# Dealing the closing products by a weight for each kind of attention slot, in place of equal shares of each step

## The reference, cut to what matters

```python
def sample_mixers(...):                       # 8 sequences, 4 new tokens each, 8192 past keys in 64 pages of 128
    o_a = dsa_attend(qa, qi, wi, qpos, kidx_all, gather_a, topk)      # branch A: keys chosen by an index score
    s = einsum('bqhmd,bshmd->bhmqs', q, k)    # branch B: scores of all past keys ...
    p = softmax(s); a = p[:, :, 0] - lam * p[:, :, 1]
    o = einsum('bhqs,bshe->bqhe', a, v)       # ... and the sum over all past values

def layer_out(h, o_a, o_b, g_a, g_b, p_i, tail):          # the closing products, for every token
    merged = sigmoid(g_a) * (o_a @ w_br_a) + sigmoid(g_b) * (o_b @ w_br_b)
    h = h + rmsnorm(merged @ w_out, attn_post_g)
    gate, up = split(rmsnorm(h, ffn_pre_g) @ w_gate_up, 2)
    h = h + rmsnorm((silu(gate) * up) @ w_down, ffn_post_g)
    return h + sigmoid(h @ w_ple_gate) * (p_i @ w_ple_proj)
```

## Time and profile before

| | |
|---|---|
| median of 3 runs | 3071.83 us (3071.17 to 3082.03) |
| the profiled execution, its own time | 3076.28 us |
| its span | 3074.7 us |
| PE busy | 2809.1 us, 91% of the span |
| DVE, ACT, POOL busy | 1398.5, 588.3, 676.6 us |
| granted TensorE clock, mean | 0.967 |
| woven stage | from about 1050 us to the end |

### The profile page before, as it was taken

The page is one execution under the profiler, slowest core; times in us unless marked ns, Lnnn a source line. Parts: engine busy times, 40 slices in busy tenths (PEclk is TensorE's granted clock), DMA queues, the critical chain, the costliest instruction groups (busy, mean ns, idle before and its releaser), DMA issues.

```text
span 3074.7 us, 69131 instructions
## 1 busy us (share of the span) xinstructions
PE 2809.1 (91%) x26846; PEld 1974.9 (64%) x26846; DVE 1398.5 (45%) x2685; ACT 588.3 (19%) x1285; POOL 676.6 (22%) x1190
## 2 busy tenths in 40 slices
PE   7998979999888598999988999999889899999898
PEld 5774434566566466667766666666666666776798
DVE  2336858997577545434344453343334532102211
ACT  2441113100566301101011110011110201001101
POOL 0131002100300000133333343433324334430000
PEclk9999989999899899999999999999899999999999
DMA  6566229521600576899898988988999987664586
GB/s 223 167 203 209 83 68 328 169 70 63 221 12 8 151 245 218 269 337 308 306 347 293 332 297 300 325 301 304 308 316 321 305 306 243 219 224 130 195 269 202
DMA packets 411138, 706.88 MB, mean 230 GB/s; under 512 B 67745, under 2 KB 225665, under 8 KB 410690
## 3 DMA queue, kind: packets, MB, share of 16 engines
q1 hardware_dynamic: 325042, 468.81, 46.3%
q0 software_dynamic: 75456, 232.86, 22.6%
q10 hardware_dynamic: 10320, 0.84, 0.3%
HBM read 659.90 MB, written 90.40 MB: 244 GB/s over the span
## 4 chain that ended last, share of the span: by engine, by line
PE 52%; DMA 4%; issue 3%; DVE 2%; ACT 1%; SPq 1%; POOLq 1%; DVEq 1%; POOL 0%; ACTq 0%
PE sa_t L1614 40%; PE sa_s L1969 4%; PE sa_o L2032 3%; DMA sa_ring_va<-cache_a_kv 2%; PE sa_s L1979 1%; PE sa_stat L2009 1%; ACT sa_prob_t L2110 1%; PE sa_o L2036 1%; DMA tw_x<-gate_t 1%; POOLq L1911 1%; DMA tw_w<-packed 1%; PE sa_t L1584 0%; DVE tw_rstd L1689 0%; DVEq L1697 0%; DMA sa_ring_k<-cache_b_kv 0%
## 5 line engine op out<-in xcount | busy, mean ns | idle before, releaser
L1614 PE MATMUL sa_t<-tw_z,tw_w 128*128 128x304 f32 (+1 forms) x3328 | 783.2, 393 | 7.2 <-issue 3.2
L1614 PEld LDWEIGHTS sa_t<-tw_z,tw_w 128*128 128x128 f32 x3328 | 572.3, 192 | 189.8 <-issue 42.3
L1912 POOL DMA_DIRECT2D sa_ring_v<-cache_b_kv x512 | 275.2, 537 | 1113.0 <-PE sa_o L2036 759.1
L1614 PE MATMUL sa_t<-tw_x,tw_w 128*128 128x304 f32 (+1 forms) x1920 | 453.0, 393 | 22.8 <-DMA tw_w<-packed 13.0
L2149 DVE STREAM_TRANSPOSE sa_key_b<-sa_ring_k 128x2048 f32<-128x2048 f32 x128 | 295.0, 2307 | 267.7 <-PE sa_s L1969 202.7
L1614 PEld LDWEIGHTS sa_t<-tw_x,tw_w 128*128 128x128 f32 x1920 | 330.9, 192 | 126.9 <-issue 32.5
L1913 POOL DMA_DIRECT2D sa_ring_va<-cache_a_kv x512 | 274.1, 535 | 54.1 <-issue 24.5
L462 PE MATMUL pr_acc<-pr_w,pr_u_t 128*128 128x512 f32 (+1 forms) x640 | 258.9, 549 | 5.2 <-DVE pr_row L651 5.2
L978 PE MATMUL sel_g<-sel_u,sel_gw 128*128 128x352 f32 x768 | 227.5, 459 | 0.0
L978 PEld LDWEIGHTS sel_g<-sel_u,sel_gw 128*128 128x128 f32 x768 | 145.8, 190 | 81.9 <-issue 0.8
L1969 PE MATMUL sa_s<-sa_key_b,sa_q_pad 32*32 32x256 f32 x8192 | 181.8, 392 | 4.9 <-issue 4.9
(11 more groups left out here) (327 smaller groups left out, 3035.1 us busy)
## 6 DMA issues: line engine op xcount, KB each, us to landing
tw_w<-packed SPq DMA_DIRECT2D x336, 512.0 KB, 5.4
sa_ring_k<-cache_b_kv SPq DMA_DIRECT2D x512, 256.0 KB, 5.7
sa_ring_v<-cache_b_kv POOLq DMA_DIRECT2D x512, 256.0 KB, 6.2
sa_ring_ka<-cache_a_kv SPq DMA_DIRECT2D x512, 64.0 KB, 5.5
sa_ring_va<-cache_a_kv POOLq DMA_DIRECT2D x512, 64.0 KB, 6.1
packed<-w_gate_up POOLq DMA_DIRECT2D x44, 512.0 KB, 12.4
tw_w<-packed SPq DMA_DIRECT2D x32, 384.0 KB, 4.5
gate_t<-sel_gate SPq DMA_DIRECT2D x16, 528.0 KB, 3.0
```

The costliest lines, as they stand in the source:

```text
L1614: ins = pe.matmul(out, self.w[:, at % self.SLOTS, first + k - lo, :], moving[:, k, cols], start=(k == 0), stop=(k == depth - 1))
L1912: pool.dma_start(ring_v[:, n % RING, :], rows_of(cache_b, page, 1)).then_inc(v_in[n // 4 % 2], 16)
```

## The change

A table gives each kind of slot a weight. The budget grows at a slot by `share` times its weight, where `share` is now the same total divided by the sum of all weights; a slot that is not in the table (`keys`, `new`, `set_q`, `evacuate`, `sum`, `finish`, `combine`) has weight 0. `LEAD`, `RESERVE`, the slots and their order, and the units and theirs are as before. The share is 15.48 for a step before, and 2.77 for a weight of 1 after: a step with neither values nor turns gets 3.5 weights, 9.7; a plain step with values 5.5 weights, 15.2; a step with 4 or 5 turns 8.3 or 9.0 weights, 23.0 or 24.9; a step with values alone, at the end, 2 weights, 5.5.

```diff
     LEAD, RESERVE = 20.0, 60.0
+    WEIGHT = {"scores": 2.0, "keys_a": 1.5, "values": 1.0, "turn": 0.7, "top": 0.5, "top_rows": 0.4, "spread": 0.4, "scores_a": 0.4}
...
-        share = (sum(costs) - LEAD - RESERVE) / len(steps)
+        share = (sum(costs) - LEAD - RESERVE) / sum(WEIGHT.get(slot[0], 0.0) for step in steps for slot in step)
...
         for step in steps:
-            for n, slot in enumerate(step):
+            for slot in step:
                 order.append(slot)
-                budget += share / len(step)
+                budget += share * WEIGHT.get(slot[0], 0.0)
                 while g < len(costs) and spent + costs[g] <= budget:
```

## The result

| | before | after |
|---|---|---|
| median | 3071.73 us (3066.77 to 3082.37, 20 runs) | 3083.24 us (3075.72 to 3093.97, 20 runs) |
| ratio, 95% interval | | 1.0036 [1.0026, 1.0046] |
| profiled execution, its own time | 3076.28 us | 3087.26 us |
| its span | 3074.7 us | 3085.7 us |

The change costs 11.5 us in the medians, 0.36%. Forecast were 3082 us and "within 0.5%". Of all timed runs of this document one was in the slow state (of `early_sized`, 4145.8 us at a granted clock of 0.65), and it is left out.

The account below looks back on a forecast made before the run. PE was taken to set the time, with transfers close behind. The terms +29 - 15 - 9 + 3 + 2 + 2 + 2 - 4 gave +10 us, forecast 3082 us (0.33% slower), own range 3066 to 3098, 8 in 10: 3050 to 3112.

Parts of the forecast that it names:

- End, +29: Steps 65 to 73: fewer units between values, so PE stands 36.9 us waiting for value pages; +29 us, bounds +20 and +38.
- Start, +3: Steps 1 to 9: scores stand closer together and keys must come at that pace; +3 us, bounds 0 and +20.
- the sign that I had named: Start of the stage: the step is wrong if scores there wait over 15 us.
- the chain's: Norm chains of the first three pieces: slots move over or out from under them; together +2 us, bounds -8 and +12.
- It fits, just: Steps 1 to 9: SP's round for keys takes 21.7 us and must fit into two steps, 26 us.
- Rival 3: First nine steps: keys come late because SP's queue is nearly full; +20 instead of +3, 3099 us, chance 0.10.
- Middle, -15 for values: Middle: more work between uses of a half removes waits for value pages; -18 + 3 = -15 us, bounds -18 and -8.
- Middle, -9 for turns: Middle: turns or `sum` directly behind a turn fall from 41 to 28, 0.72 us each; -9 us, bounds -10 and -6.
- the forecast's -24: Middle: the gain from fewer waits on value pages, -15 us, and on ACT's copies for turns, -9 us, taken together.
- Clock, -4: Half clock after waits: the middle gives back about 8 us, the end loses 4; together -4 us, bounds -20 and +16.
- rival 2: Chunks 56 to 63: the clock falls and isn't hidden, 20 instead of 4, pages later, +8; 3106 us, chance 0.28.
- The sum: Whole kernel: all terms together +10 us on a span of 3074.7, giving 3084.7, and 3082 us as the median.

Follow-up runs that it names:

- early_sized: The changed kernel with the first ten steps given 155 us of budget by the table's weights in place of 105: 3080.9 us, ratio 1.0041 to the kernel before.
- no_refill: The changed kernel without loading the value pages of chunks 58 to 63, computing with what lies in the rings: 3054.1 us, ratio 0.9945 to the kernel before.
- the shifted pair: The kernel before and the changed kernel, each with `LEAD` 27 in place of 20: 3084.7 us (ratio 1.0032) and 3102.4 us (1.0094).
- split_va: The changed kernel with branch A's value pages of the last eight chunks issued by SP instead of POOL: 3082.3 us, ratio 1.0032 to the kernel before.
- ends_even: The changed kernel with steps 0 to 9 and 65 on back at the old budget and equal shares: 3069.0 us, ratio 0.9987 to the kernel before.

## Why the prediction was right, and where its steps were off

- **End, +29**: right in its mechanism. Idle rose by 23.3 us, and `no_refill` gives back 29 us in the medians. The page waits are 25.6 us in 10 rather than 36.9: on PE the pauses were partly filled because the work between them ran at half clock (4.95 and 1.89 us where full clock has 4.36 and 1.06), so part of the cost came as clock. The pace of POOL was read rightly: the 6.06 us of a half repeat to the hundredth. The landing was not: it took 3.4 and 3.7 us after the last issue where the earlier trace rows have 5.1, a single case that I had taken for all. The Trainium skill's figure ("DMA: Bandwidth & Descriptors", "Anatomy of one DMA — SWDGE (gpsimd) path") gives an estimate of 2.6 us for a POOL page. The 3.4 to 3.7 us of this stretch lie nearer to it than the 5.1 do.
- **Start, +3**: the step that failed; the start measured +14.3 of idle, and the sign that I had named came true (scores waited 17.5 us, over 15). 7.4 us of them belong to another term: the chain's, where I wrote that the transposes come behind the reciprocal of `n2`. That happened (1183.24), while the wait behind `n1` shrank from 9.46 to 4.64. The other 10.1 us are what "It fits, just" had as +3. That sum has a landing of 1.1 us, from the issue of 1242.09 to the transpose of 1243.49. But the two belong to different halves. The transpose waited for the half before, whose last page was issued at 1234.29 and landed 9.2 us later. Before, the issue of 1234.29; then landing times of the key pages issued from 1230 to 1235, and of all from 1100 to 1240 us:

```profile
1234.29 0.33 SPq L1924 DMA_DIRECT2D sa_ring_k<-cache_b_kv  x1
DMA to landing us min/median/max: 4.5/5.4/9.2
DMA to landing us min/median/max: 2.6/3.8/9.2
```

  No page landed in less than 2.6 us. With the median of 3.8 in place of 1.1 the round of 21.7 us is 24.4 of 26, and with 9.2 it is 29.8: it doesn't fit each time. Rival 3, keys late because SP's queue is full, had this place and mechanism at +20, with a chance of 0.10; what it lacked is the landing and DVE's own order. Another 5.4 us, which no term had, went into waits of the first products for DVE (L1673 and L1676: 8.5 -> 13.9). With 105 us of budget there is too little work between, with 130 enough.
- **Middle, -15 for values**: the waits fell by 8.7 us in the window of the earlier trace rows. At equal budgets the spacing alone was worth -6.1, -17.9 and +1.5 us, and more budget with the old rule brought a gain too, which I had not counted. Taken over the whole stage the page waits went from 25.7 to 34.9 us, +9.2, where the terms for middle and end have +14.
- **Middle, -9 for turns**: right, in number and size. Over the whole stage 41 waits of a turn or `sum` became 28, as counted from the order, and 29.0 us became 19.9. In the list of 1240 to 2600 us, besides and its counterpart above, before and then after:

```profile
PE sa_stat L2005 <- ACT sa_prob_t L2110: 4.1, 6, 0.7
PE sa_stat L2016 <- ACT sa_prob_t L2110: 4.0, 6, 0.7
```

```profile
PE sa_stat L2006 <- ACT sa_prob_t L2111: 1.4, 2, 0.7
PE sa_stat L2017 <- ACT sa_prob_t L2111: 1.4, 2, 0.7
```

- **Middle, the rest**: idle there fell by 26.6 us. In the same windows (1288 to 2629 before, 1257 to 2695 after) the values' waits fell from 23.7 to 10.7 and the turns' from 25.6 to 17.1, 21.5 of it. The other 5 us lie in smaller waits. That this sum came near the forecast's -24 is partly luck of position: by the shifted pair 7 us of lead move the middle by 10 and 20 us, and counts can't tell which way.
- **Clock, -4**: busy time +2.2 us in all, where the forecast had a gain. The windows 2695 to 2740 and 2757 to 2800 us have it:

```profile
2695.00:2740.00 45.00, 33.64 (x368) 24.46 (x371) 1.32 (x5) 0.83 (x2) 28.21 (x53) 0.89 0.72 239
2757.00:2800.00 43.00, 30.17 (x328) 21.26 (x317) 0.95 (x2) 2.94 (x5) 25.75 (x48) 0.84 0.76 239
```

At 0.89 and 0.84, with PE standing 11.4 and 12.8 us, rival 2's mechanism is there, at a price that the middle's own gain in clock nearly paid back.
- **The sum**, +10 against +14.0 in the profiled executions: start 11 too small, clock 6 too small, middle 7 and the ends 7 too large. It came out near because errors of both signs met.
- **The sign** holds at the two positions that were run: after was slower than before with the lead at 20 (1.0036) and at 27 (1.0094 / 1.0032 = 1.0062), and start and end cost the same in both (+14.3 and +12.7, +23.3 and +24.3 us of idle).

## What to carry to other kernels

Filler (here the units of the closing products) that is moved between regions is paid for where it leaves. Ask at each end of a woven stage how much work the round trip of a ring (release, issue and landing) needs over it, and don't go below that. Here 130 us of budget were enough for the first ten steps and 105 were not, and 115 were nearly enough for the last ten (18.4 us of idle against 13.4) and 67 were not. When you read a landing off a timeline, make sure that the issue and its user belong to the same page. Before a planner's rule is judged by 0.3%, shift its list by one unit and time that as well: here the same rule moved by 0.3 to 0.6% when little but its position changed. Compare waits at equal budgets and over all lines that show the same cause: the largest line of the turns alone hides that 41 waits became 28. A wait that is the largest in its list need not be worth its size: taking away 17.5 us of key waits here gave back 1.4.

## What the runs showed that I had not expected

- A shift of 7 us of lead turned 9.2 us of waits for weight tiles into 29.4, with the landing time of a tile unchanged (8.0 and 8.2 us median).
- Taking two fifths of its work off POOL's queue (`split_va`, 0.92 us a page in place of 1.52) shortened the end by only 4.7 us of idle, since the landing grew from 3.4 and 3.7 to 4.3 and 5.6 us.
- Profiled executions lay up to 13 us off their kernel's median (`ends_even` 3057.3 against 3069.0, `split_va` 3069.6 against 3082.3), more than the whole effect: the regions' idle is comparable, a single total isn't.
